# A two-layer decoder trunk on one core: no products with zero states and keys, four waits elsewhere, and an ending by rows of tokens

## What is computed

```python
# layer 0: sliding-window attention, blocks of 128 queries; each block sees its own keys and the 128 before
tp = jnp.pad(t, ((0, 0), (W, 0), (0, 0), (0, 0)))          # in front of block 0 stand zero keys,
valid = (rel >= 0)[None] & (rel < W)[None] & (gkey >= 0)    # and gkey < 0 is masked away
# layer 0, beside it: RWKV-7, token by token
S_t = S_{t-1} diag(decay_t) + (S_{t-1} a_t) b_t^T + v_t k_t^T ;  y_t = S_t r_t ;  S_0 = 0
# layer 1: gated linear attention, chunk by chunk
o_inter = (q_i * exp(b)) @ state ;  o = o_inter + o_intra   # state = 0 in the first chunk
# both layers: cross-attention to 256 memory tokens, then a mixture of 32 experts (top 2 of one group)
y = zeros.at[buf_tok].add(expert_out * gate) ; x = x + y
# at the end
out = x * rsqrt(mean(x * x, axis=-1) + 1e-6) * norm_final
```

## Time and profile before

| | us |
|---|---|
| median of 3 runs | 1916.44 |
| lowest, highest | 1915.33, 1916.66 |
| profiled execution, its own time | 1916.96 |
| its span, first to last instruction | 1915.2 |
| PE busy in it | 1868.0 |

### The profile page before, as it was taken

How to read it: one execution, slowest core, us unless ns; L and a number is a source line. 1 busy time by engine, 2 the same in 40 slices (tenths; PEclk the granted TensorE clock), 3 DMA queues, 4 the chain that set the end, 5 groups by cost and what they waited for, 6 DMA issues and landing times.

```text
span 1915.2 us, 21829 instructions
## 1 busy us (share of the span) xinstructions
PE 1868.0 (98%) x8178; PEld 933.1 (49%) x8178; DVE 573.8 (30%) x1045; ACT 465.9 (24%) x813; POOL 177.2 (9%) x216
## 2 busy tenths in 40 slices
PE   8999999999999999999999999999999999999997
PEld 4555888646463333333334443686453333333333
DVE  2254556332141322313223103312241322313223
ACT  4254333242331111111113014323331111111112
POOL 2000333030100000000001000121100000000001
PEclk9999999999999999999999999999999999999998
DMA  6210100035089999999995113104089999999992
GB/s 188 88 45 6 40 1 1 23 117 193 0 314 423 423 425 423 422 423 423 424 423 212 46 44 109 67 1 179 0 321 422 424 424 422 423 423 424 423 424 117
DMA packets 88415, 465.77 MB, mean 243 GB/s; under 512 B 22304, under 2 KB 24464, under 8 KB 47403
## 3 DMA queue, kind: packets, MB, share of 16 engines
q1 hardware_dynamic: 77600, 450.98, 58.1%
q0 software_dynamic: 4608, 7.92, 1.1%
q10 hardware_dynamic: 6154, 6.15, 1.0%
HBM read 467.59 MB, written 6.29 MB: 247 GB/s over the span
## 4 chain that ended last, share of the span: by engine, by line
PE 81%; DMA 11%; DVE 4%; ACT 1%; POOL 1%; issue 1%; SPq 0%; DVEq 0%; ACTq 0%; POOLq 0%
PE ps L1040 74%; DMA W<-in_moe_w 11%; PE ps L1248 2%; PE ps L1711 1%; PE ps L1682 1%; DVE memN L1835 0%; DVE XI L2023 0%; PE ps L1185 0%; PE ps L1472 0%; DVE XJ L1964 0%; PE ps L1053 0%; DVE gcs L2132 0%; DVE KKt L1997 0%; DVE XT L2304 0%; DVE gsn L2163 0%
## 5 line engine op out<-in xcount | busy, mean ns | idle before, releaser
L1040 PE MATMUL ps<-W,xgT 128*64 128x512 f32 x2048 | 453.9, 595 | 6.3 <-DMA W<-in_moe_w 5.0
L1040 PE MATMUL ps<-HT,W 128*128 128x512 f32 (+2 forms) x896 | 337.7, 534 | 5.1 <-DVE XT L1842 1.7
L1040 PEld LDWEIGHTS ps<-W,xgT 128*64 128x64 f32 x2048 | 143.7, 137 | 287.1 <-issue 272.0
L1040 PEld LDWEIGHTS ps<-HT,W 128*128 128x128 f32 (+1 forms) x896 | 166.5, 189 | 164.4 <-issue 148.5
L2291 DVE TENSOR_TENSOR XT<-ps,XT 128x512 f32<-128x512 f32 x240 | 166.0, 692 | 239.6 <-PE ps L1040 239.6
L1040 PE MATMUL ps<-W,act 128*64 128x512 f32 x1024 | 231.9, 596 | 0.0
L1040 PE MATMUL ps<-spread,ysb 128*128 128x512 f32 x512 | 228.3, 599 | 2.2 <-issue 2.2
L1040 PEld LDWEIGHTS ps<-spread,ysb 128*128 128x128 f32 x512 | 94.8, 190 | 135.2 <-issue 134.8
L2283 DVE TENSOR_TENSOR act<-ps,sl 128x256 f32<-128x256 f32 x64 | 26.9, 420 | 446.0 <-ACT sl L991 446.0
L1040 PEld LDWEIGHTS ps<-W,act 128*64 128x64 f32 x1024 | 70.6, 137 | 133.4 <-issue 133.4
L987 ACT ACTIVATE hs<-ps 128x512 f32<-128x512 f32 x64 | 38.2, 597 | 387.2 <-PE ps L1040 387.2
(11 more groups left out here) (412 smaller groups left out, 1727.4 us busy)
## 6 DMA issues: line engine op xcount, KB each, us to landing
W<-in_moe_w SPq DMA_DIRECT2D x256, 1024.0 KB, 18.1
W<-in_moe_w SPq DMA_DIRECT2D x64, 2048.0 KB, 19.2
W<-in_od_w_in SPq DMA_DIRECT2D x6, 2048.0 KB, 8.7
W<-in_ev_w_in SPq DMA_DIRECT2D x3, 2048.0 KB, 8.0
W<-in_xa_wq SPq DMA_DIRECT2D x2, 2048.0 KB, 8.9
W<-in_xa_wo SPq DMA_DIRECT2D x2, 2048.0 KB, 12.0
hrows<-hk ACTq DMA_DIRECT2D x8, 512.0 KB, 11.8
W<-in_od_w_out SPq DMA_DIRECT2D x2, 2048.0 KB, 10.3
```

Of the source, the lines that this page charges most:

```text
L1040: return te.matmul(o, l, r, start=first, stop=last)
```

## The change

It has seven parts.

1. **Attention block 0** works on its own 128 keys alone: scores, softmax, transposes and products with values are halved, and POOL no longer makes the zero keys and the second mask.
2. **RWKV chunk 0** leaves out the products with `Sn` (four into `AKV`, four into the output), and its wait for `ck_sn`.
3. **GLA chunk 0** leaves out the 8 products with `gsn`.
4. **RWKV waits**: `BT` signals `ck_el` itself and `KT` a new semaphore `ck_kt`, for which PE waits behind the transposes of `BT`; `cumulate` stands ahead of level 1 on DVE; `decays` stands after level 3 on ACT, ahead of the copy to `AKV`.
5. **Memory tokens**: DVE scales 3, 3 and 2 of the 8 tiles ahead of additions 5, 6 and 7.
6. **cross(1)**: ACT takes heads 0 and 1 to `xo` ahead of take_turned(3).
7. **The ending**: the last pair is added as rows of tokens. For each tile t of 128 tokens PE transposes `XT` into two banks (8 transposes) and adds two products of `spread` with `ysb` onto them; ACT squares the 1024 columns with a running sum and takes the root; DVE takes the reciprocal and multiplies by it and by `fin` (the final gain on all partitions, loaded ahead of the trips by ACT's queue), half by half; SP stores 8 times 256 KB.

```diff
                     for j in range(4):
                         for g in range(2):
                             r = slice(64 * g, 64 * g + 64)
-                            ins = mm(ps[:, 4 + 2 * g + j // 2, 256 * (j % 2):256 * (j % 2) + 256],
-                                     sqT[r, j, b * P:b * P + P], skT[r, b * P:b * P + 2 * P])
+                            ins = mm(ps[:, 4 + 2 * g + j // 2, 256 * (j % 2) + own:256 * (j % 2) + 256],
+                                     sqT[r, j, b * P:b * P + P], skT[r, b * P + own:b * P + 2 * P])
...
-                    for i in range(16):
+                    for i in (range(16) if b else range(1, 16, 2)):
...
-                            for half in range(2):
+                            for half in (range(2) if b else (1,)):
...
                 def open_chunk(c):
                     turn_chunk(c, 1)
+                    pe.wait_ge(s["ck_kt"], c + 1)
                     pe.wait_ge(s["ck_y_in"], c + 1)
...
-                            pe.wait_ge(s["ck_sn"], c + 1)
-                            for j in range(4):
-                                ins = part(ps[:, 3, j * P:j * P + P], AR[:, j, 0, :], Sn[...], False)
+                            if c:
+                                pe.wait_ge(s["ck_sn"], c + 1)
+                                for j in range(4):
+                                    ins = part(ps[:, 3, j * P:j * P + P], AR[:, j, 0, :], Sn[...], False)
...
-                        mm(o, gv[:, c, e * P:e * P + P], gat[:, e // 2, :], True, False)
-                        ins = mm(o, gsn[...], gq[:, e // 2, t], False, True)
+                        ins = mm(o, gv[:, c, e * P:e * P + P], gat[:, e // 2, :], True, c == 0)
+                        if c:
+                            ins = mm(o, gsn[...], gq[:, e // 2, t], False, True)
...
                         g.tensor_tensor(AR[:, :, 0, :], KKt[:, :, t], Epp[:, :, :], ALU.mult)
-                        g.tensor_tensor(BT[:, :, :], At[:, :, t], Em[:, :, :], ALU.mult)
+                        g.tensor_tensor(BT[:, :, :], At[:, :, t], Em[:, :, :], ALU.mult).then_inc(s["ck_el"], 1)
                     if following:
-                        g.tensor_tensor(KT[:, :, :], Kt[:, :, t], Em[:, :, :], ALU.mult).then_inc(s["ck_el"], 1)
+                        g.tensor_tensor(KT[:, :, :], Kt[:, :, t], Em[:, :, :], ALU.mult).then_inc(s["ck_kt"], 1)
...
                 def memory(mt):
-                    if mt == 5:
-                        norm(memT, memN, MEM, "mem_norm", 0)
+                    if mt >= 5:
+                        norm(memT, memN, MEM, "mem_norm", 0, MEMORY_AT[mt - 5])
...
+            def last_rows(trips, pairs):
+                def turn_tokens(t):
+                    for k in range(KD):
+                        te.matmul(ps[:, ROW_BANK[t] + k // 4, P * (k % 4):P * (k % 4) + P], XT[:, k, t * P:t * P + P], ident[:, :],
+                                  start=k % 4 == 0, stop=False, is_transpose=True, skip_group_check=True)
+                def add_tokens(t):
+                    for h in range(2):
+                        ins = te.matmul(ps[:, ROW_BANK[t] + h, :], spread[:, t * P:t * P + P], ysb[:, 512 * h:512 * h + 512],
+                                        start=False, stop=False, skip_group_check=True)
+                    ins.then_inc(s["f_summed"], 1)
...
+            st.then(sc.activation(xrs[:, 0:1], cst[:, 0:1], ACT.Sqrt))
+            for t in range(TT):
+                act.wait_ge(s["f_summed"], t + 1)
+                st.then(sc.activation(osb[...], ps[:, ROW_BANK[t]:ROW_BANK[t] + 2, :], ACT.Square, accum_out=xss[:, t:t + 1]))
+                sc.activation(xrs[:, t:t + 1], xss[:, t:t + 1], ACT.Sqrt, bias=cst[:, 0:1], scale=1.0 / D).then_inc(s["row_root"], 1)
...
+            dve.wait_ge(s["fin_in"], 16)
+            for t in range(TT):
+                dve.wait_ge(s["row_root"], t + 2)
+                st.then(ve.reciprocal(srec[:, t:t + 1], xrs[:, t:t + 1]))
+                for h in range(2):
+                    half = slice(512 * h, 512 * h + 512)
+                    ve.scalar_tensor_tensor(osb[:, t, half], ps[:, ROW_BANK[t] + h, :], srec[:, t:t + 1], fin[:, half],
+                                            ALU.mult, ALU.mult).then_inc(s["f_taken"], 1)
```

More of the change, by code:

```diff
@@ L898, in cross, with take_head @@
                     take(mv[:, 1, :])
-                take_turned(3)
-                for h in range(4):
+                def take_head(h):
                     act.wait_ge(s["sm_pv"], 4 + 4 * L + h + 1)
                     sc.activation(xo[:, h, :], ps[:, (n["proj"] + h) % 2, :], ACT.Copy).then_inc(s["sm_out"], 1)
+                for h in range(2 * L):
+                    take_head(h)
+                take_turned(3)
+                for h in range(2 * L, 4):
+                    take_head(h)
                 n["xt"] += 8
@@ L1006, in pair_of_blocks @@
                     take_y(0, i)
+                if L:
+                    act.dma_start(fin[:, :], a["norm_final"].unsqueeze(0).broadcast_to([P, D])).then_inc(s["fin_in"], 16)
                 pair_of_blocks(0, first=True)
@@ L1829, in _, with norm @@
                 ve.tensor_copy(XT[:, k, :], ps[:, k, :]).then_inc(s["xt_ready"], 1)
-            def norm(src, dst, width, gain, first):
-                n["norm"] += 1
-                dve.wait_ge(s["rstd_ready"], n["norm"] - 1)
-                for k in range(KD):
+            def norm(src, dst, width, gain, first, tiles):
+                if tiles[0] == 0:
+                    n["norm"] += 1
+                    dve.wait_ge(s["rstd_ready"], n["norm"] - 1)
+                for k in tiles:
                     ve.scalar_tensor_tensor(dst[:, k, :], src[:, k, :], col(gain, first + k), rs[:, 0:width], ALU.mult, ALU.mult).then_inc(s["h_ready"], 1)
```

161 lines of the change are left out of this document (68 added, 93 removed).

## The result

The changed kernel takes 1905.12 us (median; 1898.91 to 1905.97), the kernel before 1916.44 in the same set: a ratio of 0.9926 with a 95% interval of 0.991 to 0.9943. It is faster, by 0.6 to 0.9%, but 12.8 us short of the forecast of 1892.3 and outside its range. In two later sets the same kernel took 1898.9 and 1904.0, outside the range (to 1898.0) too. In the second of these sets one execution each of the kernel before, of the changed kernel (c1_after) and of b2_waits took 3278 to 3476 us at a mean granted clock of 0.55 to 0.73, and these three are left out of every median and ratio here. The profiled execution took 1905.12 too, with a span of 1903.4, so the two profiles lie 11.8 us apart in span.

What follows compares the result with a forecast made beforehand. PE, busy 1868.0 of 1915.2 us, was taken as the bound. The terms summed to -24.2, from the profiled 1916.96 to 1892.8, or 1892.3 for the median; the 8 in 10 range was 1889.0 to 1898.0.

Steps and rivals of the forecast that it cites:

- Attention block 0: First attention block: values and transposes halve (1.0 + 0.9), scores gain 0.9; sum -2.8 us.
- Products with the state: RWKV chunk 0: four products save 0.94 us, the other four only 0.2 since PE then waits for `Us`; -1.1.
- RWKV waits: RWKV chunks: PE's three waits of 1.7 us for `KT` go; -5.1 us, or -3.7 with only the semaphore's part.
- The moved sums: RWKV chunk 0: four sums on DVE delay the first placement, slowed beside POOL's masks; +0.9 us, from +0.5 to +1.6.
- The rival's harsher estimate: RWKV chunk 0: shared port locked, so the sums cost 3.0 instead of 0.9; within a 1895.8 us rival, chance 0.1.
- The clock behind the first wait: RWKV, 222 to 225 us: PE's clock fall goes with the 1.70 us wait; -1.6 us.
- the clock still falls: RWKV part: the fall stays at chunk 0's other gaps or the new 0.9 one; 1.6 more, 1893.9 us, chance 0.17.
- Memory tokens: Memory tokens: with DVE's scaling split, PE's tile 7 follows tile 6 without its 1.74 us wait; -1.7 us.
- cross(1): cross(1): `pv(2)` no longer waits 1.60 us for the copy of head 0, nor `pv(3)`; -1.7 us.
- The ending: From ACT's last copies to the end: finish at 1905.9 instead of 1915.2 us; -9.3, between -6.2 and -10.
- its form would lower the clock: Ending: transposes between products could lower PE's clock, costing 1.6 to 7.8 us; 1893.9 to 1900.1, chance 0.12.
- The weight stream: Expert stages: rival that the stream slips to 31.3 us a period, 36 us more, 1928; chance 0.03.

Runs made afterwards that it cites:

- b2_waits: Kernel before with only the moved RWKV waits (semaphores, decays, sums); 1915.2 us against 1917.0, ratio 0.9993.
- b5: Kernel before without the eight products with the zero state in RWKV chunk 0; 1921.4 us against 1915.8, ratio 1.0024.
- b7: Kernel before without the four zero-state products into `AKV` in RWKV chunk 0, the four with `RH` kept; 1917.6 us against 1915.8, ratio 1.0007.
- b3: Kernel before with all of the change but the moved RWKV waits and the ending; 1917.0 us against 1917.0, ratio 0.999.
- b6: Kernel before with all of the change but the moved RWKV waits and the ending, four zero-state products with `RH` kept; 1908.0 us against 1915.8, ratio 0.9944.
- c0_after: The changed kernel again, unedited, in a later set; 1898.9 us against 1918.1 for the kernel before, ratio 0.9907.
- a5: Changed kernel, in RWKV chunk 0 POOL's subtractions ahead of its masks and the four zero-state products with `RH` kept; 1892.5 us, ratio 0.9869 to the kernel before.
- a1: Changed kernel with the sums and decays of RWKV chunk 0 back at their old places; 1897.8 us, ratio 0.9904 to the kernel before.
- b1: Kernel before with the new ending alone; 1908.9 us against 1918.1, ratio 0.9958.
- a2: Changed kernel with all eight zero-state products of RWKV chunk 0 kept; 1896.2 us, ratio 0.9894 to the kernel before.
- a4: Changed kernel with POOL's two subtractions ahead of its four masks in RWKV chunk 0; 1897.7 us, ratio 0.99 to the kernel before.
- a7: Changed kernel with the four zero-state products with `RH` kept in RWKV chunk 0; 1895.7 us, ratio 0.9886 to the kernel before.
- a6: a5 plus five unused DVE reductions as a delay ahead of the level 1 placement in chunk 0; 1897.6 us, ratio 0.9899 to the kernel before.

## Why the prediction was wrong

The step that failed is the price of PE's new waits in chunk 0. The wait of 0.77 us for `Us` went in at its own length, the wait behind the sums at 0.9 instead of 2.17 us, and the low clock was forecast to go (-1.6) where it grew by 10.1 us in the first set. Term by term:

- **What bounds the kernel** was right: everything went by PE's time. But PE's time was taken as a fixed number of microseconds; the low clock changed it by 10.
- **Attention block 0**, -2.8: measured -2.4. Right.
- **Products with the state**, -1.1: as work and wait it is right. The uncovered copy costs 0.77 of the second 0.94, as "only 0.2 is left" said. What failed is that this wait of 0.77 us was priced at its own length; the clock behind it was not reckoned. b5 against b7 and b3 against b6 (9 us in the median, from different sets) measure what it does.
- **RWKV waits**, -5.1: right. Without low clock the distance from chunk to chunk is 39.1 us in c0_after and a5, where the kernel before had 40.9 from chunk 2 to 3: 1.8 each. What was named as late next, the placement of level 5, did not show.
- **The moved sums**, +0.9, from +0.5 to +1.6: mis-sized, and the reading was wrong, not only the number. The ratio 1.19 to 0.68 in the earlier trace rows was taken from a mean over four operations. One by one the four of rows 6 took 0.74 us twice, and 1.77 and 1.75 where they began under a mask: about 1.0 us is lost to each mask, whatever the operation's own length. Two masks were left for the sums, so the same rows give 0.5 + 2 x 1.0 = 2.5, an estimate. The placement came 2.6 us late (196.5 in a1, whose masks started 0.4 earlier) and PE stood 2.17. The rival's harsher estimate was nearer. By the rule of the Trainium skill (SBUF — State Buffer, section "SBUF: two separate sides"), that the shared port is locked for a whole instruction, that estimate was +3.0: the trace agrees, the two sums that met a mask ending 0.3 us behind it, after 1.45 and 1.42 us, and the two that met none taking 0.39.
- **The clock behind the first wait**, -1.6: this failed, and with it the prediction. The forecast was that a fall that stood behind one wait would go with that wait; in truth falls came behind both new stalls. The rival "the clock still falls" named just this, with the gap of 0.9 among its places, but priced it at 1.6, the one fall seen. The falls of the profiled execution cost 4.8 us (195 to 210) and 6.6 (225 to 245).
- **Memory tokens**, -1.7: right in the timeline, where 2.0 us are gained by 428 us. Of these 1.2 are gone again at the first expert stage; both kernels have low clock of about the same cost there (3.3 us at 530 to 550, and 3.4 at 540 to 550), and where they went was not followed. In a5, with 1.6 us of low clock, that stage gained 2.2. **cross(1)**, -1.7: -2.1, with other low clock near it in both kernels. **GLA**, -1.8: -1.7.
- **The ending**, -9.3: -9.8, shown alone by b1. Of it 1.7 is low clock in the old ending, which the term took in without naming it. The difference is in the stores, which landed in 2.0 us, where the shortest seen had been 2.7. Against the rival that its form would lower the clock: 1.00 in all of PE's part, 1887.5 to 1897.5.
- **The weight stream**: the stages took 423.2 and 421.0 us, 423.0 and 420.0 before. The first stage took 423.0 to 423.4 in twelve of the seventeen profiles and 420.1 to 420.8 in five (a2, b1, b2, b6, b7), by when the weight DMAs came into the chain. No edit goes with that, and it stays open; 2.5 us of any single profile may be this.

Taking the cost of the low clock off the span leaves 1907.1 us before, and 1885.2, 1886.7 and 1885.6 in the three profiles of the changed kernel: 20.4 to 21.9 less. The terms without the clock's come to -22.6, and to -20.9 without the 1.7 of the old ending too. So the work was reckoned to about 1 us, with the first stall's 1.3 beyond its term in it. Of low clock the forecast left 8.1 - 1.6 - 1.7 = 4.8 us, and the three profiles have 18.2, 8.2 and 18.4. That is 13.4, 3.4 and 13.6 more, where their spans fell 12.4, 3.9 and 13.0 short of the forecast: the clock is nearly the whole of the miss.

That the stalls bring the low clock in most executions is shown, by giving and taking each. Why the clock behind the same stall costs nothing in one execution and 6.6 us in another, and why b5 and b3 lose the clock once more behind a wait that cost the kernel before nothing there, is open. The length of a wait doesn't decide it: in the kernel before and in a1, b3 and b7 PE waits 0.95 to 0.97 us ahead of the second half of its first `XI,MA` (at 197.66 in the kernel before), and the granted clock stays at 1.00 to 215 us. No run here gives the rule.

## What to carry to other kernels

Where PE is busy 98% of the time, price a new wait of PE not by its length but by the slow stretch that may follow: here a wait of 0.77 us cost 5 and turned 1.9 us of removed work into a loss of some 5, while a wait of 0.97 elsewhere was followed by no low clock at all. Before taking useless work off the critical engine, ask which copy it covers; keeping the four useless products that cover one, and moving other engines' work out of each other's way, made the fastest version. Where two engines get in each other's way, read the operations one by one before taking a ratio: a mean of four hid two that lost nothing and two that lost a whole microsecond. And read a gain in more than one execution: set the granted clock beside each span, or the same kernel differs from itself by as much as the edit gives.

## What was not expected of the hardware

- A wait of 0.77 us is followed by some 10 us at or near 1.2 GHz with no long stall ahead of it in the chunk (a1, a4), by 10 to 14 with one of 1.70 or 2.17 ahead, and in c0_after by none. The 2.17 alone is followed by 3 us of it (a7) to 10 (a2), the 1.70 alone by 3 us (before) or none (b7).
- In b3_rest twelve executions went from 1906.8 to 1923.4 us, with a mean granted clock of 0.992 in the fastest and 0.985 to 0.986 in the slowest four: 17 us in one kernel.
- A scan of 128x128 on DVE takes 0.38 to 0.43 us alone and 1.42 to 1.45 when it begins under one of POOL's two-operand masks of 128x512: it ends 0.3 us behind the mask. A reduction of 128x512 with one operand (a6) takes 0.68 to 0.69 with POOL's subtractions or mask beside it, first to last.
- A table load on ACT took 1.28 us in the ending and lay wholly under PE's first sum.
- Half stores of 256 KB, some 1.2 us apart, land in 2.0 us; whole ones of 512 KB close together took 2.7 to 5.7.
